# Adding the keys of both directions on VectorE for the diagonal of the scores, in a bidirectional HGRN2 and Conformer block

## The reference, cut to what matters

```python
def forget_gate(pre, lb):
    s = jax.nn.sigmoid(pre.astype(jnp.float32))
    f = lb + (1 - lb) * s
    one_minus_f = (1 - lb) * (1 - s)                 # the key k
    return one_minus_f, jnp.log(jnp.maximum(f, F_MIN))

# gla_scan: S_t = diag(f_t) S_{t-1} + k_t v_t^T,  o_t = S_t^T q_t
o_f, s_f = gla_scan(q, k_f, v, lf_f, s0_f)
o_b, s_b = gla_scan(flip(q), flip(k_b), flip(v), flip(lf_b), s0_b)
return o_f + flip(o_b), s_f, s_b
```

## Time and profile before

| what | value |
|---|---|
| median of 3 runs | 1431.02 us (1429.6 to 1432.42) |
| the profiled execution, its own time | 1437.04 us |
| its span, first to last instruction | 1435.2 us |
| PE busy | 1373.4 us, 96% |
| PEld busy | 1150.1 us, 80% |
| VectorE busy | 770.9 us, 54% |
| ScalarE busy | 382.3 us, 27% |
| GpSimd busy | 317.5 us, 22% |
| mean granted clock of TensorE | 0.979 |

### The profile page before, as it was taken

One profiled execution on the slowest core, in us unless ns is written; L12 is line 12 of the kernel. 1 busy time (PEld: TensorE's weight loads), 2 busy tenths in 40 slices (PEclk: granted clock), 3 DMA queues, 4 the chain that ended last, 5 costly groups with the idle time before them and its releaser, 6 DMA issues. The chain is left out here.

```text
span 1435.2 us, 17676 instructions
## 1 busy us (share of the span) xinstructions
PE 1373.4 (96%) x6805; PEld 1150.1 (80%) x6805; DVE 770.9 (54%) x976; ACT 382.3 (27%) x576; POOL 317.5 (22%) x137
## 2 busy tenths in 40 slices
PE   6899999999999988899989999999999999999998
PEld 2688888888888867687768888888888888888876
DVE  1798798888869799629622323223231313233227
ACT  3711322322222236426621111211111111211122
POOL 0521210111011151504532212212212122212110
PEclk8999999999999998999999999999999999999999
DMA  9361311230110020023321111211111111111132
GB/s 365 152 206 30 104 60 45 61 101 29 44 49 26 15 103 1 0 88 128 123 59 30 59 52 37 59 45 44 58 29 58 58 44 44 58 42 46 58 124 112
DMA packets 94715, 102.08 MB, mean 71 GB/s; under 512 B 3118, under 2 KB 77091, under 8 KB 94658
## 3 DMA queue, kind: packets, MB, share of 16 engines
q1 hardware_dynamic: 94658, 101.32, 21.1%
HBM read 92.92 MB, written 8.39 MB: 71 GB/s over the span
## 5 line engine op out<-in xcount | busy, mean ns | idle before, releaser
L1302 POOL TENSOR_TENSOR slot<-slotraw,slot 128x1024 fp32r<-128x1024 f32 x66 | 160.3, 2444 | 522.4 <-ACT slot L1238 309.9
L598 PE MATMUL bank<-h2Ta,slot 128*128 128x512 f32 x1056 | 247.5, 394 | 5.2 <-POOL slot L1302 4.9
L598 PE MATMUL bank<-slot,mid 128*128 128x512 f32 x1056 | 242.9, 391 | 1.8 <-POOL slot L1302 1.8
L598 PEld LDWEIGHTS bank<-h2Ta,slot 128*128 128x128 f32 x1056 | 200.4, 190 | 47.8 <-POOL slot L1302 5.3
L598 PEld LDWEIGHTS bank<-slot,mid 128*128 128x128 f32 x1056 | 199.3, 189 | 43.9 <-POOL slot L1302 2.2
L598 PE MATMUL bank<-cathi,slot 128*128 128x512 f32 x704 | 220.2, 389 | 0.0
L1521 DVE SCALAR_TENSOR_TENSOR cat<-conv_u,taps,cat 128x784 f32<-128x784 f32 (+29 forms) x120 | 150.1, 1251 | 10.2 <-DVE cat L1521 4.9
L598 PEld LDWEIGHTS bank<-cathi,slot 128*128 128x128 f32 x704 | 132.1, 188 | 27.8 <-issue 0.3
L1805 DVE TENSOR_TENSOR mid<-bank,sgm 128x512 f32<-128x512 f32 x44 | 30.4, 691 | 224.3 <-ACT sgm L1253 224.3
L598 PE MATMUL bank<-hT,ringb 128*128 128x512 f32 (+1 forms) x672 | 148.9, 378 | 0.0
L1830 DVE TENSOR_TENSOR arena<-bank,arena 128x512 f32<-128x512 f32 x144 | 99.5, 691 | 90.0 <-PE bank L598 89.5
(11 more groups left out here) (180 smaller groups left out, 1520.4 us busy)
## 6 DMA issues: line engine op xcount, KB each, us to landing
mraw<-in_w_mod SPq DMA_DIRECT2D x48, 512.0 KB, 6.2
slotraw<-in_ffn_w_gate SPq DMA_DIRECT2D x22, 512.0 KB, 3.7
slotraw<-in_ffn_w_up SPq DMA_DIRECT2D x22, 512.0 KB, 3.7
slotraw<-in_ffn_w_down SPq DMA_DIRECT2D x22, 512.0 KB, 4.2
ringinb<-in_w_in SPq DMA_DIRECT2D x12, 512.0 KB, 3.7
xst<-in_x SPq DMA_DIRECT2D x8, 512.0 KB, 12.8
ringina<-in_w_in SPq DMA_DIRECT2D x8, 512.0 KB, 3.7
ringinc<-in_w_in SPq DMA_DIRECT2D x8, 512.0 KB, 4.2
```

Of the source, the lines that this page charges most:

```text
L598: return pe.matmul(o, l, r, start=start, stop=stop, skip_group_check=True)
L1302: return pool.tensor_tensor(lo, full, hi.bitcast(F32), ALU.subtract)
```

## The change

The level-0 products read a sum of the two directions' keys. VectorE writes that sum, `K[:, 0, CTX:] + K[:, 1, CTX:]`, 1024 elements on 128 partitions, into `AT` right behind the two operations that make `K`, after a wait for their end, and signals `k_sum`. PE waits for `k_sum` instead of `k_ready` before level 0 and runs one product a chunk instead of two. ScalarE then overwrites `AT` with the scores, half by half, as before. VectorE's wait for PE's level 0 before its first product on `K` becomes a wait for its own `k_sum`.

```diff
@@ use(h, i) on TensorE
-                        pe.wait_ge(k_ready, h * NK + 1)
+                        pe.wait_ge(k_sum, h + 1)
...
                         if l == 0:
-                            tk = CTX + ch * P
-                            mm(o, K[:, 0, tk:tk + P], qraw[:, ch * P:(ch + 1) * P], True, False)
-                            ins = mm(o, K[:, 1, tk:tk + P], qraw[:, ch * P:(ch + 1) * P], False, True)
+                            ins = mm(o, AT[:, ch * P:(ch + 1) * P], qraw[:, ch * P:(ch + 1) * P], True, True)
@@ rec_start(h) on VectorE
                     ins = dve.tensor_scalar(K[:, d], F[:, d], sc[2], sc[1], ALU.mult, ALU.add)
                 ins.then_inc(k_ready, 1)
+                dve.wait_ge(k_ready, h * NK + 1)
+                dve.tensor_tensor(AT[:], K[:, 0, CTX:], K[:, 1, CTX:], ALU.add).then_inc(k_sum, 1)
                 for d in range(2):
@@ rec_level(h, 1, 0) on VectorE
                     if l == 1:
-                        dve.wait_ge(use_full, h * NUSE + 2)
+                        dve.wait_ge(k_sum, h + 1)
```

More of the change, by code:

```diff
@@ L328, in kernel_program @@
         use_full, use_act, use_dve = sem("use_full"), sem("use_act"), sem("use_dve")
-        k_ready, kc_ready, q_ready = sem("k_ready"), sem("kc_ready"), sem("q_ready")
+        k_ready, kc_ready, q_ready, k_sum = sem("k_ready"), sem("kc_ready"), sem("q_ready"), sem("k_sum")
         state_done, sq_ready, rs_ready, conv_done = sem("state_done"), sem("sq_ready"), sem("rs_ready"), sem("conv_done")
```

## The result

The changed kernel is slower. Its median of 11 runs is 1443.01 us (1437.17 to 1445.43), that of the kernel before in as many runs beside it 1433.65 us (1429.6 to 1436.32). The ratio is 1.0056, with a 95% interval of 1.0042 to 1.0070, or 6 to 10 us; the two medians lie 9.4 us apart. The forecast was 1438.5 us, from 1432.8 to 1442.5, against the 1431.0 us known then: 7.5 us more. The kernel before, measured beside the changed one, took 2.6 us more than it did then; applied to the 1431.0 us the ratio gives 1439.0 us, inside the range, while the median itself, 1443.01 us, is 0.5 us above its end.

The account below looks back on a forecast made before the run. VectorE's path to the small addition sets PE's next start, and VectorE bounds the tail. Delays of 2.8 us in heads 0 to 2, 1.3 in the tail and 3.4 of clock make 7.5 us: 1431.0 to 1438.5 us, range 1432.8 to 1442.5.

Parts of the forecast that it names:

- What bounds it: PE busy 96%, but its 1.6 us wait for VectorE's small addition behind rec_start matters; in the tail VectorE bounds.
- What is removed: Level 0 on PE: half of 32 rows go, 1.87 us a head, 7.5 us in four.
- What is added: One addition on VectorE in rec_start, 1.23 us plus 0.04 us for its wait: 1.27 us a head.
- PE's idle times: PE's waits for the small addition before unit 1: 2.1, 4.7 and 3.2 us in heads 0, 1 and 2.
- Heads 0 to 2: Unit 1 on PE begins later by 0.2, 1.3 and 1.3 us, and the 2.8 us delay stays.
- The tail: Head 3, where VectorE has no gap: ends 1.3 us later, with 1.0 to 1.9 us possible.
- up to 0.6 us on top: In the tail, one more VectorE operation alternating with GpSimd delays the chain by up to 0.6 us more.
- the 1.9 us: Tail cost if VectorE blocks for whole instructions beside GpSimd, by the skill's rule: 1.9 us rather than 1.3 us.
- The clock: PE's clock falls behind the longer idle times of heads 1 and 2, 1.7 us each: 3.4 us.
- the upper price of 2.75: Loss per clock fall, taken from PE's half speed behind the idle 6.26 us in the tail: 2.75 us.
- The rival that the clock holds: Same delays on PE and VectorE, no clock fall: 4.1 us slower, 1435.1 us; chance 0.20.
- The sum: Whole kernel: 4.1 us of delays plus 3.4 us of clock, 7.5 us slower, 1438.5 us.

Follow-up runs that it names:

- e3: Kernel before, with the small addition that PE awaits moved in front of the bounding of F: ratio 0.9981 to the kernel before.
- e4: Changed kernel, with the small addition that PE awaits moved in front of the bounding of F: ratio 0.9949 to the kernel before.
- e1: Changed kernel, but PE still runs both level-0 products on K; the sum is made and awaited, not read: ratio 1.0039 to the kernel before.
- e2: Kernel before with one level-0 product a chunk, on the forward keys alone, and no sum on VectorE: ratio 1.0021 to the kernel before.
- e8: Changed kernel measured again, unaltered, on another chip: ratio 1.0072 to the kernel before.
- e5: Changed kernel plus 8 or 12 unread products on PE behind level 0 in heads 0 to 2: ratio 1.0041 to the kernel before.
- e6: Changed kernel with the head in the tail as before, two products and no addition: ratio 1.0046 to the kernel before.

## Why the prediction was right

- **What bounds it.** Right. The wait of 1.6 us on one small addition was the row that mattered; e3 and e4 show it from the other side.
- **What is removed.** 1.87 us a head predicted, 3.73 - 1.95 = 1.78 by the rows. Predicted worth: nothing. e1 and e2 bear it out.
- **What is added.** 1.27 us a head on VectorE's path predicted. In head 1 the operation on `F` began 1.72 us behind `K` before and begins 2.99 us behind it now, 1.27 us more; in the tail it is 1.26. (In head 0 the sum itself is held up, beside a subtraction of GpSimd: 3.29 us, and not 1.2 as forecast, while L1539 no longer is.) From the start of `K` to the end of the small addition it was 13.17, 11.15 and 12.78 us before and is 14.42, 12.27 and 14.41 after: 1.25, 1.12 and 1.63 more. The differences from 1.27 come from which operation stands beside one of GpSimd's. In head 1 it was L1541 before and is L1539 now, and that gives 0.15 us back; in head 2 `K` is held up by 0.36 us more. The rows of head 1, first before, then after:

```profile
275.51 1.80 DVE L1539 TENSOR_SCALAR F<-F,lb 128x1280 f32<-128x1280 f32 x2
277.34 3.73 DVE L1541 TENSOR_SCALAR F<-F 128x2560 f32<-128x2560 f32 x1
...
276.25 3.88 DVE L1539 TENSOR_SCALAR F<-F,lb 128x1280 f32<-128x1280 f32 x2
280.16 1.49 DVE L1541 TENSOR_SCALAR F<-F 128x2560 f32<-128x2560 f32 x1
```

- **PE's idle times.** 2.1, 4.7 and 3.2 us predicted, 1.77, 4.24 and 3.13 measured.
- **Heads 0 to 2.** 0.2 + 1.3 + 1.3 = 2.8 us predicted; 0.29 + 0.88 + 1.27 = 2.4 in e1, where the clock held. Head 1 is the term that was too large: the chain grew by 1.12 us there, and VectorE began `rec_start` 0.26 us earlier relative to PE than before, since it had not followed the 0.26 us that PE lost in head 0. The prediction had VectorE follow PE in full.
- **The tail.** 1.3 us predicted, 1.13 measured. The prediction named L1543 as the operation that would be drawn into GpSimd's stretch, and it was, 3.27 us instead of 1.23; but the last pair, L1576, was let go in return, 3.44 us where it had been 5.58 (531.57 us in the kernel before). The two cancel to 0.1 us, and the up to 0.6 us on top did not come. The Trainium skill ("SBUF — State Buffer", "Who interferes with whom") is right about the blocking of that one operation; the 1.9 us that I had worked out with it are not what the chain lost.
- **The clock.** A fall in heads 1 and 2 and none in head 0, at 1.7 us each, predicted from idle times above and below 2.37 us. So it was in the profile: 126.34 - 124.73 = 1.61 and 116.97 - 115.35 = 1.62 us against e1. In e8 both falls cost more, 2.69 and 2.76 us, close to the upper price of 2.75. The reason for the choice did not hold: the clock fell behind 1.88 us in e2 and 2.25 us in e5, and held behind 2.46 us in e1 and 3.13 us in e6. That the right two heads fell, at the right price, is in part luck of this execution. The rival that the clock holds is what e1 shows in its own profile; for the changed kernel, the spread of its runs (1437 to 1445 us) fits some executions in which it holds and some in which it does not, but that is argued: the 27 runs of the kernel before spread over nearly as much, 1431 to 1438 us.
- **The sum.** 3.6 us of delay and 3.2 us of clock are 6.8 us, 7.5 predicted. 6.2 us were behind by level 2 of the tail, counted from the span's start, and 0.5 us the changed kernel had been ahead before head 0, for reasons outside the change. The runs without the profiler say 8.0 us (6 to 10). Both falls at the price that e8 shows would give 3.6 + 5.4 = 9.0 us.

## What to carry to other kernels

Before taking work off the busiest engine, look at what ends its next wait. Here PE was busy 96% of the time, and yet in the three bodies its next projection needed one signal that came 1.6 us late in one head and at most 1.2 us early in the others. That signal needed 0.15 us of VectorE and stood behind more than 10 us of other work in the same queue; moving that one instruction forward turned a loss of 0.6% into a gain of 0.5%, of which the move alone, without the change, is 0.2% (e3). An operation put into a queue delays all signals behind it, so a signal that another engine waits for belongs ahead of the work that nobody waits for yet.

## What was not expected of the hardware

Taking work away from PE and adding none anywhere made the kernel slower by 0.2% (e2), and with useless work for PE a part of it was faster by 1.6 us in the one execution profiled (e5). What makes the difference is the granted clock behind the idle time: the same 24 products took 5.7 us at the full clock, and 7.3 to 8.6 us where PE had been idle 1.9 to 4.4 us and the clock had fallen to half (1.2 GHz). The length of the idle time does not settle it: behind 1.88 and 2.25 us it fell (e2, e5), behind 2.46 us in e1 it held, and head 2 gave three results behind the same 3.13 us, 7.36 us in the changed kernel and the following in e8 and in e6:

```profile
411.81 8.50 PE L598 MATMUL bank<-hT,ringa 128*128 128x512 f32 x24 [3.13 <-DVE mod L1429]
...
412.01 5.74 PE L598 MATMUL bank<-hT,ringa 128*128 128x512 f32 x24 [3.13 <-DVE mod L1436]
```

The price goes with the moment of the fall. In the four places where the 24 products took 8.4 to 8.6 us, the last 2 us of the idle time already show a granted clock of 0.71 to 0.82; in the four where they took 7.3 to 7.4 us, the clock was at 1.00 up to the end of the idle time and fell when PE had begun again. The first line is of e8, 2 us before the end of the idle time in head 2, the second of e6 behind it:

```profile
409.81:411.81 2.00, 0.00 (x1) 0.01 (x1) 1.94 (x4) 0.91 (x1) 0.00 (x0) 0.76 0.00 0
...
412.01:414.01 2.00, 2.00 (x9) 1.66 (x10) 1.49 (x1) 0.00 (x0) 0.00 (x0) 1.00 0.00 0
```

What sets that moment, no run here shows.
